# One layer of a hybrid diffusion step: first modulation in row form, projection to shared expert in one block, last sums on PE

## The reference, cut to what matters

```python
# cond is c for the latent tokens and c_ctx for the context tokens: two rows
shift1, scale1, gate1, shift2, scale2, gate2 = split(silu(cond) @ w_ada + b_ada, 6)   # w_ada 1024 x 6144
h = x * (1 + scale1) + shift1
z = h @ w_in                                   # columns for RWKV-7, attention, S5, three gates
y_a, s_rwkv = rwkv_branch(za, p, state_rwkv)   # two directions, starts from the given state
y_b, y_c = attention(...), s5_branch(...)
merged = sum_n((y_n @ w_branch_n) * sigmoid(zg_n))
x = layer_norm(ALPHA * x + gate1 * (merged @ w_out), ln1_g, ln1_b)
h = x * (1 + scale2) + shift2
scores = sigmoid(h @ router_w)                 # 64 experts in 8 groups, 4 groups and 8 experts chosen
gates  = 2.5 * scores[chosen] / sum(scores[chosen])
y = sum over the 8 chosen e of gates_e * (silu(h @ w_gate_e) * (h @ w_up_e)) @ w_down_e
y = y + (silu(h @ sh_w_gate) * (h @ sh_w_up)) @ sh_w_down
x = layer_norm(ALPHA * x + gate2 * y, ln2_g, ln2_b)
```

## Time and profile before

| what | value |
|---|---|
| three runs | 2447.72, 2449.23, 2452.38 us; median 2449.23 |
| profiled execution, its own time | 2446.09 us |
| its span, first to last instruction | 2444.3 us |
| granted TensorE clock, mean | 0.893 of full |
| busy: PE, DVE, ACT, POOL | 2001.1, 931.0, 491.9, 685.3 us |
| DMA moved | 358.31 MB, mean 147 GB/s |

### The profile page before, as it was taken

How to read it: one execution, slowest core, us unless ns; L and a number is a source line. 1 busy time by engine, 2 the same in 40 slices (tenths; PEclk the granted TensorE clock), 3 DMA queues, 4 the chain that set the end, 5 groups by cost and what they waited for, 6 DMA issues and landing times. The chain is left out here.

```text
span 2444.3 us, 41126 instructions
## 1 busy us (share of the span) xinstructions
PE 2001.1 (82%) x16339; PEld 1523.5 (62%) x16339; DVE 931.0 (38%) x1863; ACT 491.9 (20%) x928; POOL 685.3 (28%) x1030
## 2 busy tenths in 40 slices
PE   7989869997878999999999947965749999999700
PEld 7665545655456777787777837733448788778500
DVE  0743213113824544444454433533332222222277
ACT  0211112202022333333333212100102122221100
POOL 4316100000004333332233213222014444444423
PEclk9999878798889999999999968987769999999955
DMA  7233333537305121222111038401039998999572
GB/s 244 62 120 95 121 112 126 197 133 255 102 24 140 32 61 55 61 59 61 41 41 30 19 104 281 147 17 57 0 145 332 337 312 308 339 339 348 189 318 99
DMA packets 244754, 358.31 MB, mean 147 GB/s; under 512 B 38306, under 2 KB 173237, under 8 KB 240773
## 3 DMA queue, kind: packets, MB, share of 16 engines
q1 hardware_dynamic: 216734, 299.42, 36.2%
q0 software_dynamic: 24560, 45.27, 5.2%
q10 hardware_dynamic: 3318, 11.59, 1.3%
HBM read 308.42 MB, written 85.65 MB: 161 GB/s over the span
## 5 line engine op out<-in xcount | busy, mean ns | idle before, releaser
L440 PE MATMUL ps_s<-hT,w_in_sb 128*128 128x512 f32 x432 | 215.9, 658 | 0.0
L2701 DVE TENSOR_TENSOR me_hh<-me_sg,ps_ju 128x128 f32<-128x128 f32 x76 | 21.9, 288 | 394.3 <-PE ps_jd L2658 371.1
L440 PEld LDWEIGHTS ps_s<-hT,w_in_sb 128*128 128x128 f32 x432 | 90.4, 216 | 105.8 <-issue 105.6
L1262 PE MATMUL ps_gs<-hT,gt_w 128*128 128x512 f32 x256 | 144.0, 645 | 7.3 <-PEq L75 7.3
L2650 PE MATMUL ps_jg<-me_xT,me_wg 128*128 128x128 f32 x1216 | 149.2, 276 | 0.0
L2650 PE MATMUL ps_ju<-me_xT,me_wu 128*128 128x128 f32 x1216 | 148.2, 275 | 0.0
L2658 PE MATMUL ps_jd<-me_wd,me_hh 128*128 128x512 f32 x304 | 143.1, 593 | 2.4 <-DVE me_yb L2707 2.4
L2650 PEld LDWEIGHTS ps_jg<-me_xT,me_wg 128*128 128x128 f32 x1216 | 142.9, 193 | 0.1
L2650 PEld LDWEIGHTS ps_ju<-me_xT,me_wu 128*128 128x128 f32 x1216 | 141.9, 192 | 0.0
L2679 ACT ACTIVATE me_xT<-ps_jx 128x1024 f32<-128x1024 f32 x77 | 78.8, 1024 | 252.0 <-PE ps_jx L2641 252.0
L1957 POOL TENSOR_TENSOR rc_lj<-rc_l,rc_lev 128x256 f32<-128x256 f32 x100 | 73.0, 750 | 179.2 <-PE ps_c L1649 178.7
(11 more groups left out here) (536 smaller groups left out, 4022.1 us busy)
## 6 DMA issues: line engine op xcount, KB each, us to landing
me_wg<-in_exp_w_gate SPq DMA_DIRECT2D x76, 512.0 KB, 5.6
me_wu<-in_exp_w_up SPq DMA_DIRECT2D x76, 512.0 KB, 7.7
me_wd<-in_exp_w_down SPq DMA_DIRECT2D x76, 512.0 KB, 5.8
cb_rows<-yj_dram SPq DMA_DIRECT2D x10, 2048.0 KB, 12.2
w_ad_sb<-in_w_ada SPq DMA_DIRECT2D x32, 512.0 KB, 4.8
w_in_sb<-in_w_in SPq DMA_DIRECT2D x31, 512.0 KB, 4.4
gt_w<-in_w_in SPq DMA_DIRECT2D x24, 512.0 KB, 4.4
zr<-in_w_ada SPq DMA_DIRECT2D x4, 2048.0 KB, 10.2
```

Of the source, the lines that this page charges most:

```text
L440: mm(ps_s[:, b, :], w_in[:, r, k, :], hT[:, k, 0:TS], start=(k == 0), stop=(k == KT - 1))
L1262: nc.tensor.matmul(ps_s[:], w[:, t % WR, k, :], hT[:, k, 0:TS], start=(k == 0), stop=(k == KT - 1))
```

## The change

- **Head.** The first modulation is made as rows: SiLU(cond) stands in the array (two columns) and 512 columns of w_ada move through it, eight multiplications for each of the four blocks into two rows of PSUM. ACT copies the 2x512 rows out, PE turns them four times per block into the same columns as before. SP's load of block j waits for block j-2 as before. ACT makes its first copy ahead of the Exp of dt and the others behind it. The RWKV start state is loaded at the head, behind w_in's first four blocks.
- **Staging.** The S5 matrices have four staging buffers in place of two.
- **Tables.** The norms stand in tau 19 and 20, the low-rank products in 21 (3), 22 (3), 23 (3), 24 (3), 25 (2), 26 (2).
- **Projection to shared expert.** One block in place of two phases. Its orders are shown below. All its weights are asked for at the start. Selection runs in three parts (tiles 0 and 1, 2 and 3, 4). The picks are made by DVE at the start of moe_phase. The one-hot matrices are built by three operations per tile (1024, 864 and 864 elements per partition), and PE multiplies a tile's as soon as they are there.
- **moe_phase.** ACT issues the loads of gate2, ln2_g and ln2_b (2 MB written) ahead of its loop.
- **Combine.** Six of the eight rows of each token are summed on PE: POOL builds six diagonal matrices of the gates per tile (768 elements per partition, two buffers), PE multiplies them with the rows (12 multiplications of 512 columns), DVE adds the other two rows, then the sum from PSUM.

The core of the diff:

```diff
-                for i in range(16):
-                    j, c = i // 4, i % 4
...
-                        last = mm(ps_ad[:, 2 * i:2 * i + 2], w_ada[:, j % 2, k, c * P:(c + 1) * P], m.c_silu[:, k, :],
+                def ada_rows(j):
...
+                        last = mm(ps_s[0:2, j % 2, :], m.c_silu[:, k, :], w_ada[:, j % 2, k, :], start=(k == 0), stop=(k == KT - 1))
+                def ada_turn(j):
...
+                        last = turn(ps_ad[:, 2 * i:2 * i + 2], adr[:, j % 2, c * P:(c + 1) * P], m.ident[0:2, 0:2])
-                    if n >= 2:
-                        act.wait_ge(at_out[n % 2], 16 * (n // 2))
+                    if n >= 4:
+                        act.wait_ge(at_out[n % 4], 16 * (n // 4))
-NORM_TAU = {18: (0, 1), 19: (2, 3)}
-LORA_TAU = {20: (0, 1, 2), 21: (3, 4, 5), 22: (6, 7), 23: (8, 9), 24: (10, 11), 25: (12, 13), 26: (14, 15)}
+NORM_TAU = {19: (0, 1), 20: (2, 3)}
+LORA_TAU = {21: (0, 1, 2), 22: (3, 4, 5), 23: (6, 7, 8), 24: (9, 10, 11), 25: (12, 13), 26: (14, 15)}
+                for t in range(NT):
+                    project(t)
+                    if t:
+                        turn(t - 1)
+                    if t >= 2:
+                        logits(t - 2)
+                logits(NT - 2)
+                shared_up(0)
+                turn(NT - 1)
+                logits(NT - 1)
+                shared_up(1)
+                pe.wait_ge(m.t_ch, len(SELECT))
...
+                def weights(t):
+                    if t >= 2:
+                        pool.wait_ge(m.e_mm, 2 * (t - 1))
+                    nc.gpsimd.tensor_tensor(diag[:, t % 2], m.ident[:].unsqueeze(1).to_broadcast([P, BYPE, P]),
+                                            m.gj[:, t, 0:BYPE].unsqueeze(2).to_broadcast([P, BYPE, P]), ALU.mult).then_inc(m.e_dg, 1)
+            @block.tensor
+            def _(pe):
+                for t in range(NT):
+                    pe.wait_ge(m.e_dg, t + 1)
+                    if t >= 2:
+                        pe.wait_ge(m.e_sum, t - 1)
+                    for j in range(BYPE):
...
-                    for j in range(TOPK):
+                    for j in range(BYPE, TOPK):
...
+                    V.tensor_tensor(x, x, ps[:, t % 2], ALU.add).then_inc(m.e_sum, 1)
```

More of the change, by code:

```diff
@@ L232, in overlay_free @@
             eng.wait_ge(m.s_vt_out, 64)
-            for n in range(2):
-                eng.wait_ge(at_out[n], 16 * 8)
+            for n in range(4):
+                eng.wait_ge(at_out[n], 16 * 4)
         def last_z_out(tau):
@@ L594, in _ @@
                 last.then_inc(m.s_dt, 1)
+                for j in range(1, 4):
+                    ada_evict(j)
                 act.wait_ge(m.s_sin, 1)
@@ L2394, in _, with project @@
                 mm = nc.tensor.matmul
-                pe.wait_ge(m.t_w, 16)
-                for t in range(NT):
+                def project(t):
+                    if t >= 2:
+                        pe.wait_ge(m.o_tp, t - 1)
+                    for h in range(2):
+                        for k in range(FT):
+                            last = mm(ps_o[:, t % 2, ts512(h)], mT[:, k, t * P:(t + 1) * P], wo[:, k, ts512(h)],
+                                      start=(k == 0), stop=(k == FT - 1))
+                    last.then_inc(m.o_mm, 1)
@@ new lines, in turn @@
+                def turn(t):
+                    pe.wait_ge(m.o_h2, t + 1)
+                    for h in range(2):
+                        if t:
+                            pe.wait_ge(m.o_ht, 2 * t + h - 1)
+                        for k in range(4):
+                            last = nc.tensor.transpose(ps_t[:, h, k * P:(k + 1) * P],
+                                                       h2[:, t % 2, (4 * h + k) * P:(4 * h + k + 1) * P], m.ident[:])
+                        last.then_inc(m.o_t_mm, 1)
@@ L2397, in _, with logits @@
+                def logits(t):
+                    if t == 0:
+                        pe.wait_ge(m.t_w, 16)
+                    pe.wait_ge(m.o_ht, 2 * t + 2)
                     for k in range(KT):
                         last = mm(ps[:, t, :], m.h2T[:, k, t * P:(t + 1) * P], rw[:, k, :], start=(k == 0), stop=(k == KT - 1))
-                last.then_inc(m.t_mm, 1)
-                pe.wait_ge(m.u_w, 32)
-                for w, done in ((wg, m.u_g), (wu, m.u_u)):
-                    if w is wu:
-                        pe.wait_ge(m.u_sg, 1)
-                    for o, sl in ((pg[:, 0, :], slice(0, TS)), (pg[:, 1, 0:TP], slice(TS, N))):
+                    last.then_inc(m.t_mm, 1)
@@ L2406, in _, with shared_up @@
+                def shared_up(c):
+                    if c == 0:
+                        pe.wait_ge(m.u_w, 32)
+                    pe.wait_ge(m.o_tp, NT - 1 + c)
+                    for n, w in ((0, wg), (1, wu)):
                         for k in range(KT):
-                            last = mm(o, w[:, k, :], m.h2T[:, k, sl], start=(k == 0), stop=(k == KT - 1))
-                    last.then_inc(done, 1)
-                pe.wait_ge(m.u_wd, 16)
-                pe.wait_ge(m.u_hh, 1)
+                            last = mm(pg[n, c], w[:, k, :], m.h2T[:, k, halves[c]], start=(k == 0), stop=(k == KT - 1))
+                    last.then_inc(m.u_up, 1)
@@ L2425, in _ @@
                 last.then_inc(m.t_cnt, 1)
[L2427 to L2429 removed]
+                pe.wait_ge(m.u_wd, 16)
+                pe.wait_ge(m.u_hh, 2)
+                for t in range(NT):
+                    for h in range(2):
+                        n = 2 * t + h
+                        if n >= 2:
+                            pe.wait_ge(m.u_acc, n - 1)
+                        mm(ps_o[:, 1, ts512(h)], hh[:, t * P:(t + 1) * P], wd[:, ts512(h)], start=True, stop=True).then_inc(m.u_dn, 1)
+                for t in range(NT):
+                    pe.wait_ge(m.t_hot, t + 1)
+                    for j in range(TOPK):
+                        q = t * TOPK + j
+                        last = mm(ps_j[:, 0:JCOLS], hot_p[:, q, :], hot_j[:, q, :], start=(q == 0), stop=(q == NT * TOPK - 1))
                 last.then_inc(m.t_tid, 1)
@@ L2479, in _ @@
[L2479 to L2487 removed]
+                link = Chain(dve, m.o_dve)
@@ L2489, in _ @@
+                for t in range(NT - 1):
+                    residual(t)
+                    if t:
+                        modulate(t - 1)
+                select(0)
+                residual(NT - 1)
+                modulate(NT - 2)
+                modulate(NT - 1)
+                select(1)
+                select(2)
+                dve.wait_ge(m.t_ch, len(SELECT))
                 link(V.tensor_tensor(gates[:], chosen[:], sc[:], ALU.mult))
@@ L2715, in group @@
                             rows(i - 1, JG - 1)
+                plink = Chain(dve, m.j_pick)
+                for t in range(NT):
+                    last = V.tensor_tensor(pick[:, t], m.slot[:, t].unsqueeze(1).to_broadcast([P, TOPK, E_N]),
+                                           m.top[:, t].unsqueeze(2).to_broadcast([P, TOPK, E_N]), ALU.is_equal)
+                plink(last)
+                for t in range(NT):
+                    last = V.tensor_tensor(pick[:, t], pick[:, t], m.gates[:, t].unsqueeze(1).to_broadcast([P, TOPK, E_N]), ALU.mult)
+                plink(last)
+                V.tensor_reduce(m.gj[:], pick[:], AX.X, ALU.add)
                 end = run(dve, group)
```

423 lines of the change are left out of this document (208 added, 215 removed).

## The result

| | before | changed |
|---|---|---|
| median of 4 runs | 2448.61 us | 2298.86 us |
| lowest, highest | 2447.72, 2452.38 | 2296.09, 2305.05 |
| profiled execution, its span | 2446.09, 2444.3 | 2296.09, 2294.2 |
| granted clock, mean | 0.893 | 0.931 |

What follows compares the result with a forecast made beforehand. PE's own work was taken as the floor, busy 2001.1 of 2444.3 us. Terms −15 − 62 + 6 − 42.5 + 3.5 − 26.5 sum to −136.5, giving 2309.6 us profiled, 2313 us against the median; range 2285 to 2344.

Steps and rivals of the forecast that it cites:

- Head: First modulation as rows: first block at the lower clock, later ones at the higher, first hT at 55 us; gain 15 us.
- Rival 1: Head: the clock stays at its lower level despite the row form, so the head gains nothing, 2328 us; chance 0.25.
- S5 and state tiles: z tiles 6 to 9, 14 to 16 and 17 lose their waits and slow instructions: gains 20.3, 20.5 and 21.5, together −62 us.
- Tables: Norms and low-rank products start a tile later, three to a tile, with ACT's store wait less hidden: +6 us, 0 to +14.
- Rival 3: Stores bind the S5 tiles, or the low-rank waits come twice: +20 us, 2333 us; chance 0.10.
- Residual to router: Projection to MoE: counts 23 us earlier, picks −9, one-hot matrices −1, their products −9.5; together −42.5 us, from −30 to −50.
- Rival 6: Router: the selection waits for a late buffer and the chain keeps its length, 2355 us; chance 0.04.
- MoE: MoE stage: 2 MB more through busy DMA and DVE's picks ahead of its first job cost +3.5 us, 0 to +10.
- Rival 5: MoE loop falls out of step behind ACT's broadcast loads; at 2.0 us per job the kernel takes 2465 us; chance 0.02.
- Combine: Combine: PE sums six rows, POOL's chain sets 28.7 us per two tiles; gain 26.5 us, 17 to 43.
- Rival 2: Combine: PE runs at the lower clock level behind its waits, so no gain there, 2339 us; chance 0.10.
- rival 4: Combine: POOL does not bind, 11.2 us a tile, 12 us better, 2301 us; chance 0.07.

Runs made afterwards that it cites:

- h_cols: The changed kernel with the first modulation made as columns again, start state still loaded at the head: 2321.69 us.
- s_two: The changed kernel with two staging buffers for the S5 matrices in place of four: 2347.25 us.
- s_sin17: The changed kernel with the RWKV start state loaded in tile 17 again, behind the S5 stores: 2325.60 us.
- s_tables: The changed kernel with the norms in tau 18 and 19 and the low-rank products as before from tau 20: 2316.44 us.
- r_late: The changed kernel with PE's turn of tile t behind projection t+2, logits one step later, first selection behind the last modulation: 2252.50 us, ratio 0.9196.
- c_vec: The changed kernel with gate2, ln2_g and ln2_b loaded at the start of the combine again: 2311.14 us.
- c_pool: The changed kernel with POOL building the diagonal matrices of tile t+2 ahead of its two operations on tile t: 2295.84 us.

## Why the prediction was right, and where it was off

**Head: −15, measured −15.6; 15.8 by h_cols.** The place holds, and with the row form the clock rose. The way to the number was another than forecast, and that both came to 55 us is luck. I had the first hT wait for the fourth load; in the trace PE's own work from the landing of the second load on sets it. The first block took 9.04 us, not 14.2, for the level rose in it; that saved nothing, since the second load landed at 28.06. The second block took 9.71, not 7.1. The third and fourth loads were then no limit at all (38.30 and the block behind it follow without a wait). Rival 1, the slow head, is out. The 56 us without a break of the prediction were not quite that: in the kernel before PE waited 1.41 us for the second load, at 27.75 us. By the page that I had weighed (the Trainium skill, TensorE: Matmul & The Clock Gate, Part 1) the clock follows how busy PE has been. The rows of h_cols show it at the lower level behind 54 us of work without a break, so the sentence doesn't cover this case.

**S5 and state tiles: −62, measured −62.8.** Taken apart by s_two (41.1) and s_sin17 (21.1), which add to 62.2 (both over the stretch up to the v tiles). The step that worked was to price a tile by a neighbour without the wait, and not by the wait: PE's six waits are 20.6 us, the stage moves by 41.

**Tables: +6, measured +0.8.** The mis-sized term. The wait that I named came (8.35 us on ACT), and two of 4 us more than before, yet tiles 19 to 26 take 137.2 us in place of 134.1, +3.1, and tile 18, now without norms, 12.2 in place of 14.5, which I had left out. The old tables would not have been free either: s_tables, with them, is 11.1 us slower than the changed kernel. I had compared the new tables with the old ones behind the old tile 17, whose 33 us had hidden the store that the norms wait for. So the edit is worth 11 us here and the stage stays where it was. Rival 3, stores that bind, is out for the S5 tiles; its other half, more waits for the stores of the low-rank products, came (20.6 us on ACT in place of 12.0) without its price of 20 us.

**Untouched stages: 0, measured −5.5.** 3.6 of it in the lanes. It is within what kernels with the same code there scatter by, and is not explained further.

**Residual to router: −42.5, measured −41.9.** Counts 24.3 us earlier against 23, and from the counts to the first product of the MoE 17.6 us less against 19.5 (picks, one-hot matrices and their products). Rival 6 is out. Two logits in the cycle cost 3.51 each, as priced. What I did not ask was whether the 10.02 us themselves could go. I took the cycle as fixed by DVE's chain; r_late shows that it was fixed by PE's own order, which asks for the turn one projection too early.

**MoE: +3.5, measured +4.1.** Right by luck. With the vectors' loads out of it (c_vec) the MoE took 496.1 us, no less, and the same kernel twice gave 494.6 and 502.1, so no part of the 4.1 us is shown to be the change's. Rival 5, the slower MoE, is out: clock 0.99 and 478.72 of 495 us busy.

**Combine: −26.5, measured −29.3.** The chain over POOL binds as predicted (28.4 and 29.6 us for two tiles against 28.7). The miss of 2.8 us is at the start: tile 0 was ready 12.5 us after the first piece, not 15, since PE's clock rose sooner, and the first piece landed 7.8 us after its load in place of 9.2. Rival 2 is out (0.47 us an instruction; the lower level would be some 0.89, twice 0.444), rival 4 was no case of this kernel but is what c_pool comes near to, until DVE binds.

## What to carry to other kernels

Price a wait of PE by the tile around it, not by its own length: here 20.6 us of waiting moved a stage by 41, and 34.5 us of idle time less moved another by 43, because the work behind each wait ran slowly. When a producer's chain makes PE wait once per tile, first ask whether PE asks one tile too early; here delaying the consumer by a tile cost a new order and no buffer. And when a stage gets shorter, look for the store or load that it had been hiding: the table of tiles had to move with it.
